# A transformer layer on one core: the group sums of the down projection's inner blocks move from VectorE to GpSimd

## What is computed

```python
def swiglu(x, w_gate, w_up, w_down):
    return (jax.nn.silu(x @ w_gate) * (x @ w_up)) @ w_down
...
f = swiglu(rmsnorm(h, g_ffn1_pre[i]), w_ffn1_gate[i], w_ffn1_up[i], w_ffn1_down[i])
h = h + 0.5 * rmsnorm(f, g_ffn1_post[i])
...
f = swiglu(rmsnorm(h, g_ffn2_pre[i]), w_ffn2_gate[i], w_ffn2_up[i], w_ffn2_down[i])
h = h + 0.5 * rmsnorm(f, g_ffn2_post[i])
```

## Time and profile before

| | |
|---|---|
| median of three runs | 1858.17 us |
| the profiled execution's own time | 1857.78 us |
| its span | 1856.0 us |
| TensorE (PE) busy | 1834.7 us, 99% |
| VectorE (DVE) busy | 1506.1 us, 81% |
| ScalarE (ACT) busy | 1017.5 us, 55% |
| GpSimd (POOL) busy | 113.9 us, 6% |
| first half of the first down projection | about 477 to 600 us |
| first half of the second | about 1509 to 1630 us |

### The profile page before, as it was taken

One profiled execution on the slowest core, in us unless ns is written; L12 is line 12 of the kernel. 1 busy time (PEld: TensorE's weight loads), 2 busy tenths in 40 slices (PEclk: granted clock), 3 DMA queues, 4 the chain that ended last, 5 costly groups with the idle time before them and its releaser, 6 DMA issues.

```text
span 1856.0 us, 22616 instructions
## 1 busy us (share of the span) xinstructions
PE 1834.7 (99%) x8442; PEld 1508.0 (81%) x8442; DVE 1506.1 (81%) x1712; ACT 1017.5 (55%) x1321; POOL 113.9 (6%) x162
## 2 busy tenths in 40 slices
PE   9999999999999999999999999999999999999998
PEld 7788888888877878888888888888888887788886
DVE  6788888888898888777896788888888889978765
ACT  6555555555555556555555645555555555545663
POOL 1000000000000001013551100000000000000010
PEclk9999999999999999999999999999999999999999
DMA  7766666666666655655556566666666666666654
GB/s 229 247 217 214 194 205 204 211 218 204 212 210 203 198 198 171 194 177 160 156 179 201 164 213 207 228 224 209 199 205 196 218 197 201 205 212 202 203 188 145
DMA packets 214157, 372.10 MB, mean 200 GB/s; under 512 B 16592, under 2 KB 41632, under 8 KB 213664
## 3 DMA queue, kind: packets, MB, share of 16 engines
q1 hardware_dynamic: 187440, 356.69, 59.9%
q10 hardware_dynamic: 26608, 13.96, 2.6%
HBM read 358.01 MB, written 2.10 MB: 194 GB/s over the span
## 4 chain that ended last, share of the span: by engine, by line
PE 87%; DVE 8%; DMA 3%; ACT 1%; issue 0%; ACTq 0%; SPq 0%; POOL 0%; DVEq 0%; POOLq 0%
PE bank L747 23%; PE bank L749 23%; PE bank L748 23%; PE bank L732 5%; PE bank L733 5%; PE bank L731 5%; DVE w_rest L1695 4%; DMA branch<-in_w_ffn_down 3%; PE bank L1111 1%; PE bank L853 1%; PE bank L1140 1%; PE bank L1122 1%; DVE w_rest L1682 1%; DVE branch L1701 1%; DVE branch L1704 0%; DVE branch L1703 0%
## 5 line engine op out<-in xcount | busy, mean ns | idle before, releaser
L747 PE MATMUL bank<-w_high,x_high 128*128 128x512 f32 (+1 forms) x1592 | 621.9, 391 | 3.2 <-DVE w_rest L1862 2.3
L749 PE MATMUL bank<-w_high,x_rest 128*128 128x512 f32 (+1 forms) x1592 | 616.6, 387 | 0.0
L748 PE MATMUL bank<-w_rest,x_high 128*128 128x512 f32 (+1 forms) x1592 | 616.3, 387 | 0.0
L1385 ACT CAST w_high<-raw 128x1024 fp32r<-128x1024 f32 x280 | 294.8, 1053 | 292.1 <-PE bank L749 191.2
L1862 DVE TENSOR_TENSOR w_rest<-raw,w_high 128x1024 fp32r<-128x1024 f32 x280 | 336.2, 1218 | 102.7 <-ACT w_high L1385 101.7
L747 PEld LDWEIGHTS bank<-w_high,x_high 128*128 128x128 f32 x1592 | 299.1, 188 | 66.8 <-issue 3.3
L749 PEld LDWEIGHTS bank<-w_high,x_rest 128*128 128x128 f32 x1592 | 299.0, 188 | 61.6
L748 PEld LDWEIGHTS bank<-w_rest,x_high 128*128 128x128 f32 x1592 | 299.2, 188 | 58.9
L1682 DVE TENSOR_TENSOR w_rest<-raw,w_high 128x1024 fp32r<-128x1024 f32 x166 | 204.3, 1239 | 62.0 <-ACT w_high L1254 61.3
L1254 ACT CAST w_high<-raw 128x1024 fp32r<-128x1024 f32 x166 | 172.4, 1049 | 127.2 <-PE bank L749 124.4
L1272 ACT CAST w_high<-raw 128x1024 fp32r<-128x1024 f32 x136 | 141.8, 1052 | 116.4 <-PE bank L749 106.9
(11 more groups left out here) (246 smaller groups left out, 2290.1 us busy)
## 6 DMA issues: line engine op xcount, KB each, us to landing
raw<-in_w_ffn_up SPq DMA_DIRECT2D x156, 512.0 KB, 4.9
raw<-in_w_ffn_gate SPq DMA_DIRECT2D x154, 512.0 KB, 4.5
raw<-in_w_ffn_down SPq DMA_DIRECT2D x144, 512.0 KB, 4.9
raw<-in_w_qkv SPq DMA_DIRECT2D x68, 512.0 KB, 3.9
raw<-in_w_o SPq DMA_DIRECT2D x32, 512.0 KB, 4.4
raw<-in_w_ple_gate SPq DMA_DIRECT2D x32, 512.0 KB, 4.5
branch<-in_w_ffn_down SPq DMA_DIRECT2D x30, 512.0 KB, 5.5
gain_row<-in_w_ffn_gate SPq DMA_DIRECT2D x20, 512.0 KB, 5.2
```

The lines of the kernel that those rows point to most:

```text
L747: nc.tensor.matmul(o[:, 0:width], xh, wh, start=first and c == 0, stop=False, skip_group_check=go_on)
L748: nc.tensor.matmul(o[:, 0:width], xh, wr, start=False, stop=False, skip_group_check=go_on)
L749: ins = nc.tensor.matmul(o[:, 0:width], xr, wh, start=False, stop=last and c == chunks - 1, skip_group_check=go_on)
L1385: nc.scalar.copy(w_high[:, n % RING], src).then_inc(w_high_done, 1)
```

## The change

The function `combine` leaves VectorE and becomes one loop on GpSimd, called once for each feed-forward, with the same five operations for each group. GpSimd starts group 0 when all moved blocks of the inner activation are split and TensorE has finished the slots ahead of the down projection, and groups 1 to 3 when VectorE has made `x_rest` of the group before (`comb_rest`). In the order of the slots, ScalarE's cast and `combine_rest` keep their places for groups 1 to 3 and come one slot later for group 0. GpSimd's norm factors are called around the new loop in the order in which they are needed.

```diff
-    COMBINE_AT = [0] + [at - 5 for at in GROUP_AT[1:]]
+    COMBINE_AT = [3] + [at - 3 for at in GROUP_AT[1:]]
...
+            def combine(n0, f):
+
+                for i in range(GROUPS):
+                    chunks = slice(CB * i, CB * i + CB)
+                    if i:
+                        pool.wait_ge(comb_rest, GROUPS * f + i)
+                    else:
+                        pool.wait_ge(moved_rest, f * MOVED + MOVED)
+                        pool.wait_ge(w_used, n0)
+                    step(nc.gpsimd.tensor_tensor(whole, h_high[:, chunks, :].bitcast(F32),
+                                                 h_rest[:, chunks, :].bitcast(F32), ALU.add))
+                    a11, a12 = whole[:, 0:CPS, 0:P], whole[:, CPS:CB, 0:P]
+                    a21, a22 = whole[:, 0:CPS, P:S], whole[:, CPS:CB, P:S]
+                    nc.gpsimd.tensor_tensor(mixed[:, 2], a21, a11, ALU.subtract)
+                    step(nc.gpsimd.tensor_tensor(mixed[:, 0], a21, a22, ALU.subtract))
+                    step(nc.gpsimd.tensor_tensor(mixed[:, 1], a11, mixed[:, 0], ALU.subtract))
+                    nc.gpsimd.tensor_tensor(mixed[:, 3], a12, mixed[:, 1], ALU.subtract).then_inc(combined, 1)
+
+            factors(factors_up_to(J_IN1))
+            combine(S_DOWN1, 0)
             factors(factors_up_to(J_POST1))
...
             square_pair(PAIRS - 1)
+            factors(factors_up_to(J_IN2))
+            combine(S_DOWN2, 1)
             factors(len(FACTORS))
...
-                        if j == 0 and t - 2 in COMBINE_AT:
-
-                            i = COMBINE_AT.index(t - 2)
+                        if j == 0 and t in COMBINE_AT:
+
+                            i = COMBINE_AT.index(t)
                             act.wait_ge(combined, GROUPS * f + i + 1)
...
                         if j == 0 and t in COMBINE_AT:
-                            combine(COMBINE_AT.index(t))
-                        if j == 0 and t - 2 in COMBINE_AT:
-                            combine_rest(COMBINE_AT.index(t - 2))
+                            combine_rest(COMBINE_AT.index(t))
```

More of the change, by code:

```diff
@@ L1943, in down @@
                 end = n0 + PAIR_OPS * (NBD // 2)
[L1945 to L1956, removed]
                 def combine_rest(i):
```

## The result

The changed kernel takes 1883.31 us (median of 4, 1881.21 to 1884.84), the kernel before 1858.62 on the same chip (4, 1857.96 to 1860.42): a ratio of 1.0129, 95% interval 1.0113 to 1.0144, **slower by 24.7 us**. Profile against profile it is 1883.58 - 1857.78 = 25.8 us. The forecast was 1880.0 in 1865 to 1889: sign and mechanism held, and 21.8 us of cost was 3 to 4 us too little.

What follows compares the result with a forecast made beforehand. A loop of VectorE sums, cast, rest of sum4 and partner's transfer, 21.64 us a turn, was taken to pace TensorE. 2.2 + 4.35 + 4.35 = 10.9 us a call, 21.8 for two, gave 1880.0 us, range 1865 to 1889.

Steps and rivals of the forecast that it cites:

- The gain from the removal is 0: Taking the 2.85 us combines off VectorE only lengthens its wait for the partner's transfer, so it saves 0.
- GpSimd's durations: On GpSimd, 2.37 us for the 1024-element addition and 0.738 for each 256-element subtraction, 5.3 us a combine if unhindered.
- The high end of 3.0: Upper estimate in us for GpSimd's 1024-element addition, which would make the kernel's time 1884 us.
- Turns, not sharing, and the waiting GpSimd gets the next one: GpSimd operations alternate with VectorE's two-SBUF-input instructions in its back-to-back stretch, costing 2.17 us per large, 0.55 per small one.
- VectorE keeps its turn: Rival: back-to-back VectorE subtractions are not broken into, GpSimd's large operation waits for a gap; +10, 1868 us, chance 0.08.
- the groups 0: Start of each down-projection call, where GpSimd makes group 1's combine: the partner's transfer and line 1701 come 2.2 us late.
- +4.35: Us added in each of groups 1 and 2 by the next group's combine in VectorE's back-to-back stretch: 2.17 + 4 x 0.55.
- The narrow bounds of the forecast: 1877 to 1886 us for alternation as worked out, chance 0.80, from the uncertainty of the terms.
- TensorE's waits: TensorE's waits for the weight rests of line 1695 in the down projections: about 28 us instead of 6.7.
- VectorE's wait for the transfer: VectorE's wait for the partner's transfer ahead of line 1701: about 3 us instead of 0.2 to 0.5.
- The rival "faster": VectorE's own load, not the transfer, holds line 1701, so removal ends six stalls: up to -6.7 us, 1852, chance 0.04.

Runs made afterwards that it cites:

- the kernel with useless additions: Kernel before, its combines still on VectorE, plus seven unused GpSimd additions of 128x240 behind each of the first three lines 1962 of a call: 1873.63 us.
- the large addition alone: Changed kernel with GpSimd making only the 128x1024 addition of each group, the four subtractions left out: 1865.82 us in one run.
- opening the loop: Kernel before, first-half partner blocks of groups 2 and 3 sent to the gain row's buffer, gains loaded later: 1855.23 us, ratio 0.9982.
- the second place for the transfer: Changed kernel, first-half partner blocks of groups 2 and 3 sent to the gain row's buffer, gains loaded later: 1874.30 us, ratio 1.0087.

## Why the prediction was right, and where it was short

**The gain from the removal is 0**: right, shown by leaving the work out (0.9994), with the 2.85 us found as waiting for the transfer.

**GpSimd's durations**: forecast 2.37 and 0.738 us; unhindered ones took 2.38 and 0.74. The high end of 3.0 was not needed.

**Turns, not sharing, and the waiting GpSimd gets the next one**: right. Forecast 2.17 and 0.55 us for a turn, measured 3.34 - 1.14 = 2.20 and 1.67 - 1.14 = 0.53; 2.20 + 4 x 0.53 = 4.3 for a combine, as measured from line 1723 to line 1728. "VectorE keeps its turn" had nothing for it: in group 1 VectorE ran back to back and was broken into five times. By the Trainium skill, SBUF — State Buffer, "SBUF: two separate sides", whichever engine comes second is blocked for the whole instruction of the other. Five whole operations of GpSimd, by their measured lengths, would be 5.3 us a combine; the measured 4.3 decides against that size, and for the page's statement that the two engines exclude each other.

**Where the forecast was short.** It was 2 x 2.2 for the groups 0 and 4 x 4.35 for the turns of the loop. Measured turns, from line 1701 or 1723 to the next:

| | before | after | more | of it up to the last sum | behind it |
|---|---|---|---|---|---|
| call 1, groups 1 to 2 | 21.64 | 26.83 | 5.19 | 4.33 | 0.86 |
| call 1, groups 2 to 3 | 21.94 | 26.99 | 5.05 | 4.34 | 0.71 |
| call 2, groups 1 to 2 | 21.59 | 27.74 | 6.15 | 4.34 | 1.81 |
| call 2, groups 2 to 3 | 22.08 | 28.03 | 5.95 | 4.34 | 1.61 |

The four turns are 22.3 us instead of 17.4: **4.9 us were missing. The term that was too small is the "+4.35" of groups 1 and 2**, which holds GpSimd's turns (they came out at 4.33) and nothing for what a longer stall does to the rest of the loop. The forecast saw TensorE's stall grow to about 5 us in all, and priced it as waiting only. What the trace shows in its place is that a stall of 3.38 us came with a granted clock at 1.2 GHz behind it, and that these slow matmuls sit inside the loop: they hold slots, ScalarE's cast waits for a slot (4.43 us in the row above), and the rest of sum4 is late by them, 1.07 us in the first call and 2.19 in the second between groups 1 and 2, of which the transfer gave 0.2 and 0.4 back. In the changed kernel itself the lower clock was not taken away. What shows its part is the two turns in the kernel with useless additions: behind equal stalls the cast comes 1.59 us later at the lower clock. In the changed kernel it comes 4.64 us behind the stall's end; 1.59 us earlier, and VectorE's waits of 0.80 and 0.16 us for casts, which make up the 1.07 with the small gaps beside them, would be gone. That is worked out, not run. With the large addition alone, longest stall 1.8 us, there is no slow stretch, and a turn of 23.86 has just the one term.

**The groups 0** cost 3.2 and 2.0 us against 2.2 each. In the first call the rest of slot 14 was late as forecast, 2.1 us; one more came from the partner's transfer, which took 7.8 us from its issue (508.86) to line 1723 instead of 6.7. At the same place of the second call it took 6.4, and in the experiments that load it there 5.9 to 8.1; why it was long here is open. Between group 3 of the first call and the second call 1.7 us were given back. So the sum closes: 4.9 more in the turns, 0.8 more in the groups 0, 1.7 given back, 4.0 in all, which is 25.8 - 21.8.

**Where luck helped.** The narrow bounds of the forecast, 1877 to 1886, take in the 1883.3, but not for their own reason. Their upper side stood for a large addition of 3.0 us (and by the prediction's own terms it ends at 1884, not 1886); the addition took 2.38, and what filled the room was the slow matmuls, for which no term stood.

**TensorE's waits**: 23.9 us, forecast 28. That is 4 us less than forecast, while the slow matmuls, in no forecast, add 8 us of busy time. VectorE's wait for the transfer was to be about 3 us and is 2.4 to 4.3. The rival "faster" had the right object and the wrong size: opening the loop did bring something, 0.2%, but taking VectorE's load away didn't open it (1857.38 us without the sums).

## What to carry to other kernels

Before moving elementwise work to GpSimd, look at what VectorE does at that moment: where it runs back to back on two-input operations from SBUF, each moved operation costs VectorE most of its length on GpSimd: here 4.3 us a combine, where VectorE itself had needed 2.85. Work that lies in a transfer's shadow is worth nothing to remove; what paces the loop is the buffer that frees the transfer, and without opening that nothing gained here. Add to a sum the price of a clock that may fall behind a new stall of 2.3 us or more, and ask whether slow matmuls hold something that the loop needs.

## What was not expected of the hardware

**Stalls and the clock.** Four stalls of 3.38 us in the changed kernel each had the lower level behind them, for 3.5 to 5.7 us. In the kernel with useless additions stalls of 3.15, 3.11 and 2.89 us had it too, but one of 3.14 us did not. Its two stretches in the first call:

```profile
527.20:530.60 3.40, 3.40 (x15) 2.80 (x16) 3.40 (x3) 0.55 (x2) 3.24 (x3) 1.00 0.89 287
551.95:556.40 4.45, 4.45 (x13) 3.48 (x14) 4.45 (x3) 0.24 (x1) 3.52 (x3) 0.62 0.80 261
```

In the changed kernel with the second place for the transfer a stall of 2.32 us had the full clock behind it and one of 2.33 us, at the same place of the second call, the lower one:

```profile
553.66:558.00 4.34, 4.34 (x19) 3.59 (x20) 4.34 (x4) 1.27 (x2) 0.44 (x1) 1.00 0.90 264
1593.31:1597.00 3.69, 3.69 (x10) 2.94 (x11) 3.69 (x3) 0.21 (x1) 0.44 (x1) 0.58 0.98 261
```

Behind the stalls of 1.8 us and less in the down projections of all kernels here it stayed at the full level. So the length of the stall alone doesn't tell it; what else does was not tested.

**Writes don't take turns.** This the experiment's theory had supposed, but no row of the kernel before showed it. GpSimd's memsets over the same tiles (2.98 us for three) left VectorE's two-input instructions at 1.22 us.
